# Latent attention with joined score products and an earlier search for the largest score, and gated norms summed over all partitions

## What is computed

```python
def mla_attention(c_q, c_kv, k_r, ...):            # 8 heads, 64 + 32 rows of keys, per layer
    q_rope = apply_rope(q[..., 64:], cos, sin)
    k_rope = apply_rope(k_r[:, :, None, :], cos, sin)[:, :, 0, :]
    s = (einsum('bqhd,bkhd->bhqk', q_nope, k_nope)      # 64 rows
         + einsum('bqhr,bkr->bhqk', q_rope, k_rope)) * 96 ** -0.5   # 32 rows, one key for all heads
    p = softmax(s)
    return einsum('bhqk,bkhd->bqhd', p, v)

def _hgrn2_mixer(...):                                  # second block, layer 0
    o = forward scan + backward scan                    # per head of 128 channels
    o = _rmsnorm(o, norm_g) * silu(g)                   # mean of squares over the head's channels

def _rwkv7_mixer(...):
    g = sigmoid(gd) @ g2                                # (512, 128) @ (128, 512)
    ...
    return (y + bonus) * g
```

## Time and profile before

| | us |
|---|---|
| median of 3 runs | 2756.87 |
| lowest and highest | 2755.76, 2760.75 |
| the profiled execution, device time | 2744.78 |
| its span, first to last instruction | 2742.8 |

### The profile page before, as it was taken

One profiled execution on the slowest core, in us unless ns is written; L12 is line 12 of the kernel. 1 busy time (PEld: TensorE's weight loads), 2 busy tenths in 40 slices (PEclk: granted clock), 3 DMA queues, 4 the chain that ended last, 5 costly groups with the idle time before them and its releaser, 6 DMA issues. The chain is left out here.

```text
span 2742.8 us, 44702 instructions
## 1 busy us (share of the span) xinstructions
PE 2559.9 (93%) x19048; PEld 2062.0 (75%) x19072; DVE 1507.2 (55%) x2230; ACT 945.3 (34%) x1419; POOL 283.0 (10%) x232
## 2 busy tenths in 40 slices
PE   8999999999999988999879896999989998999898
PEld 7888765678887666788658785788878776788786
DVE  3474387543753776446356565755455496545532
ACT  4223225433232245443444342343322323433321
POOL 0000030010000300200333130100003000000011
PEclk9999999999999999999989999899999998999999
DMA  4232223113232231223200001432325111232231
GB/s 140 93 100 92 94 95 133 62 63 100 95 98 101 93 135 49 71 92 100 82 1 4 3 4 40 177 99 93 126 105 215 62 64 62 78 106 93 87 115 52
DMA packets 56394, 238.20 MB, mean 87 GB/s; under 512 B 6592, under 2 KB 7360, under 8 KB 47616
## 3 DMA queue, kind: packets, MB, share of 16 engines
q1 hardware_dynamic: 56192, 235.30, 24.6%
HBM read 231.08 MB, written 4.19 MB: 86 GB/s over the span
## 5 line engine op out<-in xcount | busy, mean ns | idle before, releaser
L348 PE MATMUL banks<-b_h,pin_pair 128*128 128x512 f32 x2304 | 528.3, 390 | 0.0
L348 PEld LDWEIGHTS banks<-b_h,pin_pair 128*128 128x128 f32 x2304 | 431.1, 188 | 89.0
L348 PE MATMUL banks<-ffh,ff_pair 128*128 128x512 f32 x2016 | 457.3, 389 | 0.0
L348 PEld LDWEIGHTS banks<-ffh,ff_pair 128*128 128x128 f32 x2016 | 378.3, 188 | 78.7
L348 PE MATMUL banks<-b_h,pab_pair 128*128 128x512 f32 x792 | 180.7, 390 | 2.3 <-DVE pab_pair L334 2.3
L348 PEld LDWEIGHTS banks<-b_h,pab_pair 128*128 128x128 f32 x792 | 148.4, 188 | 33.4 <-DVE pab_pair L334 2.7
L2868 DVE TENSOR_TENSOR ff<-ff_c,ff 128x512 fp32r<-128x512 f32 x44 | 30.5, 692 | 204.8 <-ACT ff L2856 203.4
L334 DVE TENSOR_TENSOR pin_pair<-pin_raw,pin_pair 128x1024 fp32r<-128x1024 f32 x50 | 61.3, 1226 | 135.0 <-ACT pin_pair L327 135.0
L334 DVE TENSOR_TENSOR pin_pair<-first,pin_pair 128x1024 fp32r<-128x1024 f32 x50 | 61.3, 1226 | 126.9 <-ACT pin_pair L327 126.9
L327 ACT ACTIVATE ff_pair<-ff_raw 128x1024 fp32r<-128x1024 f32 x58 | 61.5, 1059 | 182.5 <-PE banks L348 182.5
L1220 DVE SCALAR_TENSOR_TENSOR x<-banks,modf,x 128x512 f32<-128x512 f32 x32 | 24.0, 750 | 172.7 <-PE banks L366 172.7
(11 more groups left out here) (543 smaller groups left out, 4588.2 us busy)
## 6 DMA issues: line engine op xcount, KB each, us to landing
ff_raw<-in_ffn_up SPq DMA_DIRECT2D x58, 512.0 KB, 3.7
pin_raw<-in_w_in SPq DMA_DIRECT2D x50, 512.0 KB, 3.5
first<-in_w_in SPq DMA_DIRECT2D x48, 512.0 KB, 3.5
dn_raw<-in_ffn_down SPq DMA_DIRECT2D x16, 1408.0 KB, 7.4
dil_ada_ring<-in_ada_w SPq DMA_DIRECT2D x20, 1024.0 KB, 7.0
first<-in_ffn_up SPq DMA_DIRECT2D x30, 512.0 KB, 3.8
mla_ada_ring<-in_ada_w SPq DMA_DIRECT2D x12, 1024.0 KB, 9.7
pab_raw<-in_ab_in SPq DMA_DIRECT2D x23, 512.0 KB, 3.5
```

What stands on the lines that cost most here:

```text
L348: mm = nc.tensor.matmul(bank, w(a, k), x(b, k), start=k == 0 and i == 0, stop=k == kt - 1 and i == 2)
```

## The change

In MLA, 64 and 32 rows of a head's queries and keys are laid one under the other in tiles of 96 rows, so that a unit has two score products in place of four. For this ACT moves the query tiles by halves (8 copies of 64 rows in place of 4 of 128), DVE makes the keys by halves (8 products in place of 4), and POOL copies the turned 32 rows under them (16 copies). DVE's turn u now begins with largest and shift of unit u + 1, ahead of the fold and of the scaling of unit u. PE's turn stays as it was. The first query products begin before the low half of the first weights is ready. The ring of the folds has two slots and not four.

In HGRN the norm's sums are one product with a matrix of ones (128x512), which leaves them on all partitions; a logarithm and an exponential on ACT make the inverse root, and DVE multiplies. Columns, roots, reciprocals, widened rows and their spreading go. ACT's and DVE's starts are reordered (`ends(1)` ahead of the key norms). The four gate products and their load move to the start of the first `rwkv_units`, and the ACT copies with them.

```diff
@@ mla_attention
-        qn, qr = sb("qn", [P, PAIRS, T]), sb("qr", [P, 2, T])
+        q, qr = sb("q", [P, HEADS, T]), sb("qr", [P, 2, T])
+        sooner = sb("k", [P, HEADS // 2, T])
-        ada = Modulations(nc, m, c, sem, "mla", 16 * layer + DIL_CHUNKS, 6, m.ps[:, 7])
+        ada = Modulations(nc, m, c, sem, "mla", 16 * layer + DIL_CHUNKS, 6, m.ps[:, 7], slots=2)
+        def key_rows(h):
+            return sooner[:, h] if h < HEADS // 2 else later[:, h - HEADS // 2]
                     for e in range(2):
-                        h = halves(e)
-                        nc.tensor.matmul(m.ps[:, s + e], qn[h, pair, at], kn[h, pair], start=True, stop=False)
-                    for e in range(2):
-                        r = slice(64 * e + 32 * (pair % 2), 64 * e + 32 * (pair % 2) + ROPE)
-                        mm = nc.tensor.matmul(m.ps[:, s + e], qr[r, pair // 2, at], m.kr[r], start=False, stop=True)
+                        mm = nc.tensor.matmul(m.ps[:, s + e], q[0:NOPE + ROPE, 2 * pair + e, i * P:i * P + P],
+                                              key_rows(2 * pair + e)[0:NOPE + ROPE], start=True, stop=True)
+            @block.gpsimd
+            def _(pool):
+                pool.wait_ge(turned, 1)
+                for h in range(0, HEADS, 2):
+                    if h == HEADS // 2:
+                        pool.wait_ge(fine, nq + nkv)
+                    for e in range(2):
+                        nc.gpsimd.tensor_copy(key_rows(h + e)[NOPE:NOPE + ROPE], m.kr[NOPE:NOPE + ROPE]).then_inc(roped, 1)
+                    pool.wait_ge(turned, 2 + h // 4)
+                    for e in range(2):
+                        at = 2 * ROPE * e + ROPE * (h // 2 % 2)
+                        nc.gpsimd.tensor_copy(q[NOPE:NOPE + ROPE, h + e], qr[at:at + ROPE, h // 4]).then_inc(roped, 1)
-                for u in range(units):
-                    pair, i, s = u // TT, u % TT, 2 * (u % 2)
+                def largest(u):
+                    i, s = u % TT, 2 * (u % 2)
                     dve.wait_ge(scored, u + 1)
+                    if u >= 2:
+                        dve.wait_ge(weighed, 2 * u - 2)
                     chain.step(nc.vector.tensor_reduce(top[:, u % 2], m.ps[:, s:s + 2], AX_X, ALU.max))
+                largest(0)
+                for u in range(units):
+                    if 1 <= u < units - 1:
+                        largest(u + 1)
...
+                    if u == 0:
+                        largest(1)
@@ hgrn
+                def logarithm(h):
+                    act.wait_ge(totalled, h + 1)
+                    nc.scalar.activation(root_h(h), m.ps[:, 6 + h % 2], ACT.Ln, bias=m.eps[:, 0:1], scale=1.0 / P)\
+                        .then_inc(logged, 1)
                 def root(h):
+                    act.wait_ge(logged, h + 1)
+                    nc.scalar.activation(root_h(h), root_h(h), ACT.Exp, scale=-0.5).then_inc(rooted, 1)
+                    nc.tensor.matmul(m.ps[:, 6 + h % 2], m.ones[:], sq[:, h % 2], start=True, stop=True)\
+                        .then_inc(totalled, 1)
-                    if s % 2 == 1:
-                        gate_sums(s // 2)
+                totals(2)
                 values(sets - 1)
-                pe.wait_ge(placed_r, PAIRS)
-                stretch(0)
-                stretch(1)
-                totals(2)
                 totals(3)
-                stretch(2)
-                stretch(3)
@@ rwkv_units
                 if d == 0:
                     dc.lows(pe, 0, 0, low_banks)
+                    pe.wait_ge(g2_in, 16)
+                    for i in range(PAIRS):
+                        nc.tensor.matmul(m.ps[:, 4 + i], g2[:, i * P:i * P + P], rr[:, 14], start=True, stop=True)\
+                            .then_inc(gated, 1)
                     dc.powers(act, 0, 0)
-                    dc.powers(act, 0, 1)
+                    for i in range(PAIRS):
+                        if i == 2:
+                            dc.powers(act, 0, 1)
+                        act.wait_ge(gated, i + 1)
+                        nc.scalar.activation(m.mix[:, 4 + i], m.ps[:, 4 + i], ACT.Copy).then_inc(placed, 1)
```

More of the change, by code:

```diff
@@ L860, in mla_attention @@
         low = sb("low", [P, 2, nq + nkv, T], F32R)
[L861 to L862 removed]
+        q, qr = sb("q", [P, HEADS, T]), sb("qr", [P, 2, T])
+        v, later = (raw[:, n * TT * T:(n + 1) * TT * T].rearrange("p (j n) -> p j n", j=TT) for n in range(2))
+        sooner = sb("k", [P, HEADS // 2, T])
         work = sb("work", [P, 8, T])
@@ L965, in mix, with query @@
                     mm.then_inc(used, 1)
-                for k in range(nq):
+                def query(k, t, a, b):
+                    col = HEADS * NOPE + t * P if t < 2 else (t - 2) * P
+                    return nc.tensor.matmul(m.ps[:, t], uq[:, a, k, col:col + P], low[:, b, k],
+                                            start=k == 0 and (a, b) == (0, 0),
+                                            stop=k == nq - 1 and (a, b) == (1, 0), skip_group_check=True)
+                pe.wait_ge(high, 1)
+                pe.wait_ge(lifted, 1)
+                for a, b in ((0, 0), (0, 1), (1, 0)):
+                    if b:
+                        pe.wait_ge(left, 1)
+                    if a:
+                        pe.wait_ge(fine, 1)
+                    for t in range(q_tiles):
+                        query(0, t, a, b)
+                for k in range(1, nq):
                     pe.wait_ge(fine, k + 1)
@@ L970, in _ @@
                     for t in range(q_tiles):
-                        col = HEADS * NOPE + t * P if t < 2 else (t - 2) * P
                         for a, b in ((0, 0), (0, 1), (1, 0)):
-                            mm = nc.tensor.matmul(m.ps[:, t], uq[:, a, k, col:col + P], low[:, b, k],
-                                                  start=k == 0 and (a, b) == (0, 0),
-                                                  stop=k == nq - 1 and (a, b) == (1, 0), skip_group_check=True)
+                            mm = query(k, t, a, b)
                         if k == nq - 1:
@@ L1028, in _ @@
                     act.wait_ge(made, t + 1)
-                    nc.scalar.activation(qr[:, t] if t < 2 else qn[:, t - 2], m.ps[:, t], ACT.Copy).then_inc(taken, 1)
+                    if t < 2:
+                        nc.scalar.activation(qr[:, t], m.ps[:, t], ACT.Copy).then_inc(taken, 1)
+                        continue
+                    for e in range(2):
+                        nc.scalar.activation(q[0:NOPE, 2 * t - 4 + e], m.ps[halves(e), t], ACT.Copy).then_inc(taken, 1)
                 act.wait_ge(stretched, 1)
@@ L1843, in _ @@
                 for s in range(sets):
-                    if s + 1 < sets:
+                    if 1 <= s and s + 1 < sets:
                         ends(s + 1)
@@ L1857, in _ @@
                                 .then_inc(logged_k, 1)
+                        act.wait_ge(kept, 16)
+                        logarithm(0)
                     if s == 6:
@@ L1861, in _ @@
                             nc.scalar.activation(norm_k(i), norm_k(i), ACT.Exp, scale=-0.5).then_inc(rooted_k, 1)
-                root(0)
+                        root(0)
+                square(2)
+                logarithm(1)
+                logarithm(2)
+                square(3)
+                logarithm(3)
                 root(1)
-                square(2)
                 root(2)
-                square(3)
                 root(3)
```

141 lines of the change are left out of this document (51 added, 90 removed).

## The result

| | before | changed |
|---|---|---|
| median of 4 runs, us | 2756.69 | 2847.77 |
| lowest and highest | 2755.76, 2760.75 | 2845.24, 2850.60 |
| the profiled execution, device time | 2744.78 | 2845.24 |
| its span | 2742.8 | 2843.1 |

The account below looks back on a forecast made before the run. PE, busy for 93% of the span, was taken to bound the kernel. MLA +84.2 us, HGRN -10.7 and RWKV start 0 summed to +73.5, on 2756.9 giving a forecast of 2830 us, range 2785 to 2860.

Parts of the forecast that it names:

- The sequence in the MLA loop: MLA loop: scores, search, scaling and transposes run in sequence; 15 turns take 97.3 us, 26.9 more than before.
- The clock: MLA loop: PE at half clock behind waits in six fold turns, 16.7 us more a layer, bounds 0 and 42.
- Rival 1: MLA loop: the sequence holds but the clock does not fall; +40, 2797 us; chance 0.2.
- rival 2: MLA loop: clock stays low throughout, 42 in place of 16.7 us a layer, 2881 us; chance 0.06.
- rivals 4 and 5: MLA loop: 4, the sequence breaks up, faster, 2723 us, chance 0.07; 5, gains and losses cancel, within 0.2%, chance 0.03.
- Rival 4's deciding point: MLA loop: whether the scores of u + 1 have ended when DVE finishes scaling u - 1.
- Ahead of the loop: MLA before its loop: first products start about 1.3 us sooner; 1.5 us less a layer, bounds 2 less and 3 more.
- The joined product: MLA scores: a product of 96 rows costs 0.88 us, so a unit's scores 1.76 us in place of 2.12.
- rival 3: MLA scores: the joined product costs the whole pair's 1.06 us, 0.36 more in 28 turns, 2840 us; chance 0.09.
- The ring: MLA folds: two slots cost nothing, chunks loading during over 10 us between folds of different pairs; 0 to 4 us a layer if late.
- HGRN: HGRN stage: 6.9 us won by set 5 and 3.8 in the tail; -10.7 us, bounds -5 and -14.
- RWKV start: Start of RWKV units: four gate products hide in PE's wait of 10.10 us; 0, without that cover 4 us.

Follow-up runs that it names:

- the kernel with idle products: Changed kernel plus 14 unused identity products on PE ahead of the transposes in the six MLA turns with a fold: ratio 1.0235 to before.
- the early search alone: Kernel before with only DVE's search of the largest scores moved one unit ahead, four score products kept: ratio 1.0375 to before.
- scores of u + 2: Changed kernel with PE making scores of unit u + 2, not u + 1: 0.9963; kernel before with this, early search and paired products: 0.9924.
- the part alone: Kernel before with only the HGRN and RWKV part of the change: ratio 0.9986 to before, 4 us less.

## Why the prediction was right, and where it was off

**The sequence in the MLA loop (forecast 97.3 us from first to last mix without clock loss).** Right, 2.0 us too long: 95.3 by the turns of the kernel with idle products. Its two kinds of turn are 4.98 us (forecast 5.0) and 7.88 (8.05) wherever the clock held, PE's waits 4.31 and 4.04 (4.3) behind a fold and 1.15 in plain turns (1.2). One detail was misread: the product with the gate doesn't make a turn of 6.0 of its own. The mix that waits for it stands in the same stretch from mix to mix as the fold of the turn before, so every second fold turn is 12 to 13 us and the turns around it are 4.98 to 6.3.

**The clock (forecast 16.7 us a layer).** Right in kind and about in size: 16.8 us in the first loop, 20.5 in the second, of which the idle products gave back 10.2 and 14.1. The loops took 112.1 and 115.8 us, together within 0.1 us of twice the forecast 97.3 + 16.7 = 114.0. That closeness is luck: the sequence was forecast 2.0 us too long in each loop, and the clock 0.1 and 3.8 us too cheap. Rival 1 (no fall) and rival 2 (low throughout) are out by the same rows, and rivals 4 and 5 by the time. Rival 4's deciding point, scores ready before the search, is what the kernels with scores of u + 2 made true, and they were faster.

**Ahead of the loop (forecast -1.5, bounds -2 and +3).** Wrong in sign. The first mix came 40.59 us into the stage and not 37.27, 3.3 later (3.6 in layer 1), and 0.9 came back at the end of the stage. The step that failed was the early start of the queries: it moved the first scores from 21.30 to 21.67 us into the stage, not ahead, because PE's key products wait 1.32 us (to 434.88) for ACT's copy of the inverse norm, which stands behind the longer row of query copies. The forecast had read DVE's rotation as what holds the keys; its own row has DVE waiting 0.33 us for PE's key product. Then came what I had only put into the bound. DVE and POOL in the changed kernel:

```profile
446.76 1.36 POOL L1032 COPY mla_q<-mla_qr 32x512 f32<-32x512 f32 x2 [6.70 <-DVE mla_qr L310]
446.80 1.60 DVE L1156 TENSOR_SCALAR mla_work<-mla_work,mla_total 128x512 f32<-128x512 f32 x2
...
449.56 0.55 DVE L1135 TENSOR_SCALAR mla_shift<-mla_top,mla_q_minus 128x2 f32<-128x2 f32 x1
```

```profile
452.99 3.78 PE L924 MATMUL banks<-mla_k,mla_q 96*128 96x512 f32 x4 [3.87 <-ACT mla_raw L1059]
```

Beside POOL's copies the two scalings take 1.60 us (0.88) and the shift 0.55 (0.23). With the later first search that puts unit 1's shift 1.7 us back, PE's wait grows from 1.43 to 3.87, and the scores behind it run at half clock, 3.78 us. It is the last of these that doubles the delay.

**The joined product (0.88 each).** 0.905: 1.81 us for two, from start to start of the next. The forecast's 1.76 was good, and rival 3 is out. The scores also begin 0.93 and not 1.02 us after the transposes ahead of them, so a turn gains 0.40. It does so in the closed sequence too: plain turns of 4.98 us against 5.39 with the early search alone.

**The ring (forecast 0).** Wrong, 6.6 us for the whole kernel in its own run, inside the bound of 4 a layer. The step said that chunks have more than 10 us between folds of different pairs. At PE's pace of 3.8 us a turn that isn't so: in the kernel with scores of u + 2 the first pair of chunks was free by 462.93, and the next was wanted at 468.5 and came at 471.19.

**HGRN (forecast -10.7).** -5.8 in the profile. Up to the last set's crossing 5.05 us were won (53.79 us into the stage, 58.84 before), where 6.9 by set 5 was forecast. The four waits of PE for POOL in the changed kernel are 2.51, 0.74, 0.49 and 3.03, 6.8 in all, against the 4.70 + 2.31 = 7.0 of the earlier trace rows: removing the longest moved the work up and the wait along. From the start of the last crossing to the end of the stage it is 19.9 us, where it was 20.6: 0.7 less, and 3.8 were forecast. The step that failed was to leave out the clock: the wait grew from 2.31 to 3.03, and the crossing products right behind it and all up to 7 us later ran at a mean clock of 0.58, where in the kernel before half clock began 1.4 us after the wait and lasted some 3.5 us. One gate product that had stood 12 us ahead of that wait is gone, which may be why PE now arrives earlier; no run puts it back.

```profile
1500.30:1507.30 7.00, 6.96 (x31) 6.14 (x32) 3.71 (x6) 2.58 (x3) 0.68 (x4) 0.58 0.01 4
```

**RWKV start (forecast 0).** Right: its first unit's transposes begin 13.87 us into the stage and 13.89 before, with the gate products ahead of them in the old wait of the earlier trace rows. The transposes run at half clock as before (1.08 us for four entries), but the group behind them, 1.98 us long at 1434.23 in the kernel before, is at full clock now:

```profile
1523.93 5.03 PE L2434 MATMUL banks<-b_rr,rx_y 128*128 128x512 f32 x8
1534.10 1.08 PE L2310 MATMUL banks<-ident,rx_ar 128*128 128x128 f32 x4 [5.13 <-issue]
...
1536.82 1.11 PE L2323 MATMUL banks<-rx_ar,rx_bb 64*64 64x128 f32 x32
```

**The sum.** 92.3 for MLA (forecast 84.2: 8.1 too low, nearly all of it ahead of the loop), -11.3 for HGRN and RWKV (forecast -10.7), 6.7 in other stages, which the spread between executions covers (the same stages took 1945.1 us in the kernel before and 1951.5 in the one that only adds waits in dilated attention): 87.7 us, and 91.1 between the medians. That -11.3 meets -10.7 is luck again: HGRN gave 5.8, RWKV's 5.5 stand in no term of the forecast and are mostly spread between executions, and the part alone was worth 4 us in its own run. With 4 in place of 10.7 the miss of 17.6 us (91.1 against 73.5) is the 8.1 of MLA and 6.7 here; the last 3 are within what two medians can tell. The profile's own difference of 100 us holds 12.6 more of dilated attention. The forecast noted that the median of before lay 12.1 us above its profile and left it unexplained. The long form of two sums, 6.1 and 6.4 us, is of that size, and it stands in the one trace that is known to come from the slower chip; no trace of the kernel before in that form was taken, so this is only argued.

## What to carry to other kernels

A step that is moved ahead on one engine gains nothing until its input is moved ahead too: here DVE searched one unit earlier, PE still made the scores behind the transposes that wait for DVE, and two engines that had overlapped took turns, at 87 us in the two loops. One line on PE turned the loss into a gain of 0.4%, and giving back one slot of the ring made it 0.9%. So for each moved step, follow its input back to the engine that makes it and ask whether that stands behind something that waits for the mover. And where the work in front of one of PE's waits changes, price the clock behind that wait as well.

## What the runs showed of the hardware

- These instructions of DVE and POOL keep each other out. An addition of 128x1024 on POOL takes 2.35 us alone and 8.94 beside a burst of DVE's scalar-tensor-tensor instructions of 0.41 us each, of which it let some sixteen pass by; the other way round DVE's eight took 5.34 in place of 3.24. The Trainium skill ("SBUF — State Buffer", SBUF: two separate sides) says that the shared port pair is an exclusive lock and that the one who starts first has it for a whole instruction. The trace agrees that it is exclusive, but POOL was shut out for a whole row of short instructions, 6.7 us, though its row begins while the last two of the first burst and all 14 of the second were still to come.
- A short wait can be followed by half clock: behind 1.15 us, in a loop that had waited 2.27 us 17 us earlier and 0.72 us 7 us earlier, the scores ran at half clock (3.66 us). In the kernel before, waits near 1 us were not followed by it. What makes the difference is not shown.
- A product of 96 rows and 512 columns in 32 bits takes 0.905 us, a pair of 64 rows side by side 1.06, and a pair of 32 rows also 1.06. The Trainium skill ("TensorEngine Tiling (Array Packing)", Theoretical Speedup) gives up to twice the speed for up to 64 rows, which would put a pair at the price of one; here it is 1.06 where one of 128 rows is 0.88, which is why joining 64 and 32 rows, 2.12 us in pairs and 1.81 joined, wins 0.3 us a unit against that rule.
